# Local attention's probabilities: multiplied by the reciprocal of their sums on ScalarE instead of VectorE

## The reference

```python
# sliding_window_gqa_sinks, 16 query heads of 64, 2 key heads, window 128, two blocks of 128 queries
s = jnp.where(mask[None, :, None, None], s, -jnp.inf)
m = jnp.maximum(jnp.max(s, axis=-1, keepdims=True), sink)
p = jnp.exp(s - m)
p = p / (jnp.sum(p, axis=-1, keepdims=True) + jnp.exp(sink - m))
o = jnp.einsum("bnhgqk,bnkhd->bnqhgd", p.astype(vb.dtype), vb)
```

## Time and profile before

| | us |
|---|---|
| median of 3 runs (2653.89 to 2655.39) | 2654.91 |
| the profiled execution | 2654.99 |
| its span, first to last instruction | 2653.3 |
| TensorE busy | 2593.8 (98% of the span) |
| TensorE's weight loads busy | 2282.8 (86%) |
| VectorE busy | 1715.2 (65%) |
| ScalarE busy | 1275.3 (48%) |

### The profile page before, as it was taken

How to read it: one execution, slowest core, us unless ns; L and a number is a source line. 1 busy time by engine, 2 the same in 40 slices (tenths; PEclk the granted TensorE clock), 3 DMA queues, 4 the chain that set the end, 5 groups by cost and what they waited for, 6 DMA issues and landing times.

```text
span 2653.3 us, 40305 instructions
## 1 busy us (share of the span) xinstructions
PE 2593.8 (98%) x14812; PEld 2282.8 (86%) x14812; DVE 1715.2 (65%) x2239; ACT 1275.3 (48%) x1803; POOL 28.6 (1%) x50
## 2 busy tenths in 40 slices
PE   8999999998999999999999999999999999999998
PEld 8998889888977899999999988878888888888886
DVE  5778888885886755455556565467865555555654
ACT  5656454565557444343454444454444444444443
POOL 1000000000000000000000000000000000000000
PEclk9999999999999999999999999999999999999999
DMA  6565878774675556555567776658875656666664
GB/s 208 169 206 159 272 214 246 239 232 135 201 236 190 183 178 188 168 174 185 171 210 252 248 230 194 195 186 266 284 246 184 188 186 191 186 190 189 206 192 141
DMA packets 453112, 538.62 MB, mean 203 GB/s; under 512 B 33307, under 2 KB 344118, under 8 KB 452342
## 3 DMA queue, kind: packets, MB, share of 16 engines
q1 hardware_dynamic: 449430, 522.47, 62.7%
q0 software_dynamic: 3360, 14.31, 1.7%
q10 hardware_dynamic: 192, 0.08, 0.0%
HBM read 534.66 MB, written 2.10 MB: 202 GB/s over the span
## 4 chain that ended last, share of the span: by engine, by line
PE 88%; DVE 5%; ACT 2%; DVEq 2%; issue 1%; DMA 1%; ACTq 0%; SPq 0%
PE banks L2138 21%; PE banks L2139 20%; PE banks L2141 20%; PE banks L2123 7%; PE banks L2126 7%; PE banks L2124 6%; DVE w_lo L1385 2%; PE banks L2587 1%; DMA w_raw<-in_l_w_in 1%; PE banks L2327 1%; DVEq L1376 1%; PE banks L2629 1%; PE banks L2644 1%; PE banks L2567 1%; ACT w_hi L766 1%
## 5 line engine op out<-in xcount | busy, mean ns | idle before, releaser
L1385 DVE TENSOR_TENSOR w_lo<-w_raw,w_hi 128x1024 fp32r<-128x1024 f32 (+2 forms) x840 | 975.4, 1169 | 628.9 <-ACT w_hi L766 598.3
L766 ACT ACTIVATE w_hi<-w_raw 128x1024 fp32r<-128x1024 f32 (+2 forms) x840 | 843.3, 1013 | 908.3 <-PE banks L2141 751.9
L2138 PE MATMUL banks<-w_hi,act_hl 128*128 128x512 f32 (+2 forms) x2496 | 963.0, 386 | 8.2 <-DVE act_hl L1450 2.2
L2139 PE MATMUL banks<-w_hi,act_hl 128*128 128x512 f32 (+2 forms) x2496 | 957.2, 384 | 0.0
L2141 PE MATMUL banks<-w_lo,act_hl 128*128 128x512 f32 (+2 forms) x2496 | 692.9, 383 | 0.0
L2138 PEld LDWEIGHTS banks<-w_hi,act_hl 128*128 128x128 f32 x2496 | 471.1, 189 | 99.2 <-issue 3.7
L2139 PEld LDWEIGHTS banks<-w_hi,act_hl 128*128 128x128 f32 x2496 | 472.0, 189 | 82.8 <-issue 0.2
L2141 PEld LDWEIGHTS banks<-w_lo,act_hl 128*128 128x128 f32 x2496 | 456.9, 189 | 82.9
L2123 PE MATMUL banks<-act_hl,w_hi 128*128 128x256 f32 x1696 | 444.4, 293 | 8.8 <-ACT scr_a L772 2.5
L2124 PE MATMUL banks<-act_hl,w_hi 128*128 128x256 f32 x1696 | 429.6, 284 | 0.0
L2123 PEld LDWEIGHTS banks<-act_hl,w_hi 128*128 128x128 f32 x1696 | 324.4, 191 | 20.0 <-issue 9.6
(11 more groups left out here) (317 smaller groups left out, 1600.2 us busy)
## 6 DMA issues: line engine op xcount, KB each, us to landing
w_raw<-in_od_w_in SPq DMA_DIRECT2D x256, 512.0 KB, 3.9
w_raw<-in_ev_w_in SPq DMA_DIRECT2D x256, 256.0 KB, 3.7
w_raw<-in_l_w_in SPq DMA_DIRECT2D x96, 512.0 KB, 4.3
w_raw<-in_l_w_in SPq DMA_DIRECT2D x128, 256.0 KB, 3.8
ada_ring<-in_ada_w SPq DMA_DIRECT2D x128, 256.0 KB, 4.4
w_raw<-in_l_w_out SPq DMA_DIRECT2D x64, 512.0 KB, 4.8
y_mix<-in_ada_w SPq DMA_DIRECT2D x128, 256.0 KB, 3.2
const_b<-in_ada_w SPq DMA_DIRECT2D x128, 256.0 KB, 4.7
```

The costliest lines, as they stand in the source:

```text
L766: last = nc.scalar.activation(dst(w_hi[:, p % RING, :]), src(w_raw[:, p % RING, :]), ACT.Copy)
L1385: last = tt(dst(w_lo[:, p % RING, :]), src(w_raw[:, p % RING, :]), dst(w_hi[:, p % RING, :]).bitcast(F32), ALU.subtract)
L2138: mm(out, ah, hi, start=start, stop=False, skip_group_check=True)
L2139: r = mm(out, al, hi, start=False, stop=False, skip_group_check=True)
```

## The change

For each block ScalarE first runs the exponentials of both pairs as before. Then comes a drain, and for each pair a wait for its reciprocals and four copies in place with a scale that is read per partition from `soft`: for each head one of 128x128 and one of 128x256, eight copies a block. The last one signals that the probabilities are ready. VectorE adds the sink's term and takes the reciprocals, signals them for each pair, and no longer multiplies; its two multiplies a pair, four a block, go. No DMA and no matmul is added, removed or moved in the programs.

```diff
-            "swa": ("keys", "gate", "scores", "max", "exp", "prob", "probT", "probT_sb", "o", "y"),
+            "swa": ("keys", "gate", "scores", "max", "exp", "inv", "prob", "probT", "probT_sb", "o", "y"),
...
                     for n in range(2):
                         sc.wait_ge(s["max"], 2 * i + n + 1)
                         exps(swa_s, (2 * n, 2 * n + 1), s["exp"], True)
+                    nc.scalar.drain()
+                    probs = view(swa_s, 4, 384)
+                    for n in range(2):
+                        sc.wait_ge(s["inv"], 2 * i + n + 1)
+                        for h in (2 * n, 2 * n + 1):
+                            for b, (lo, hi) in enumerate(((0, 128), (128, 384))):
+                                last = copy(probs[:, h, lo:hi], probs[:, h, lo:hi],
+                                            scale=soft[:, 4, 2 * h + b:2 * h + b + 1])
+                    last.then_inc(s["prob"], 1)
...
                         drain()
-                        last = normalise(swa_s, (2 * n, 2 * n + 1))
-                    last.then_inc(s["prob"], 1)
+                        nc.vector.reciprocal(soft[:, 4, 4 * n:4 * n + 4], soft[:, 2, 4 * n:4 * n + 4]).then_inc(s["inv"], 1)
```

## The result

The changed kernel takes 2660.07 us (median of 20 runs, 2657.68 to 2662.98); the kernel before, on the same chip, 2655.64 us (20 runs, 2653.89 to 2658.43). The ratio is 1.0016, with a 95% interval from 1.001 to 1.0022: 4.4 us or 0.17% longer. The forecast was 2659.6 us. The profiled execution took 2661.22 us with a span of 2659.3 us and a mean granted clock of 0.992.

What follows compares the result with a forecast made beforehand. TensorE, busy 98% of the span, was taken as the bound, so only its waits or clock matter. The profiled 2654.99 + 3 x 0.97 for the longer chain + 1.7 for one clock fall gave 2659.6 us, range 2657.1 to 2661.9.

Steps and rivals of the forecast that it cites:

- Where the cost is paid: TensorE's waits before the transposes grow to 2.60, 2.00 and 2.24 us in blocks 2 to 4; block 1 costs nothing.
- The copies: ScalarE's eight scaled copies a block take 2.85 us, at the exponentials' 0.30 and 0.40 us each.
- The lower bound of 2.17: Least time in us for a block's eight ScalarE copies, from copies without a per-partition scale; +0.29 us a block.
- The drain, the reciprocals and the table load: On ScalarE: copies start 0.09 us after the exponentials, reciprocals are not late, no table load (rival with loads: chance 0.02).
- +0.97 a block: Transposes in blocks 2 to 4 start 0.97 us later each, bounds +0.29 and +1.60; +2.9 us over three blocks.
- the 0.6 us wait for `w_lo` in block 2 stays: TensorE's 0.6 us wait for a weight piece in block 2 lies before the multiplies, so it does not change.
- VectorE's relief counted at nothing: Removing four multiplies a block frees VectorE but not TensorE, whose next `w_lo` needs ScalarE's later `w_hi`: 0 us.
- What queues behind: ScalarE's next `w_hi` starts 2.95 us later, yet `w_hi` and `w_lo` arrive in time, by 0.4 and 0.3 us: no cost.
- The clock: TensorE's clock halves behind the longer waits of blocks 2 to 4, about a half each; likeliest once, 1.7 us, chance 0.37.
- the row without a fall and the one with it: Earlier TensorE waits: 2.47 us before 621.69 without a halved clock, 2.17 us with clock 0.50 from 644.45 to 647.86.
- none of today's waits is followed by a fall: In blocks 2 to 4 of the kernel before, TensorE's three waits, 1.63 us at most, were followed by no halved clock.
- The sum: Whole kernel: 2654.99 + 3 x 0.97 + 1.7 = 2659.6 us, +4.6 us or +0.17%.

Runs made afterwards that it cites:

- experiment 7: The changed kernel with a constant scale of 0.125 in the eight copies instead of the reciprocals: 2657.15 us, ratio 1.0004 to the kernel before.
- experiment 9: The changed kernel with ScalarE signalling each pair of copies, so TensorE transposes the first pair during the second's copies: 2658.11 us, ratio 1.0009 to the kernel before.
- experiment 10: The kernel before with one head of the second pair copied on ScalarE and transposes by pairs: 2653.83 us, ratio 0.999; on another chip 2655.0 us, ratio 0.9994.
- experiment 3: The changed kernel with 11, 8 and 9 unread matmuls filling TensorE's waits in blocks 2, 3 and 4: 2658.01 us, ratio 1.0007 to the kernel before.

## Why the prediction was right

**Where the cost is paid: right.** The waits are 2.60, 2.00 and 2.24 us, as foreseen to 0.01. Changing block 1 alone cost nothing; doubling its copies made a wait there.

**The copies: right.** 2.87 us against 2.85, from the pitch of the exponentials with the same operand kind. The lower bound of 2.17 came from copies without the scale per partition, and such copies took 2.13 (experiment 7).

**The drain, the reciprocals and the table load: right.** 0.08 against 0.09 us; the second pair's reciprocals are there at 266.42, about 1 us before their copies start (an estimate: half of 2.87 us after 266.05); no load.

**+0.97 a block: right, but the sum over the blocks was 0.35 too large.** The step that failed is the sentence that the 0.6 us wait for `w_lo` in block 2 stays, with VectorE's relief counted at nothing. The wait does lie before block 2's multiplies, but block 1's lie before the wait. That wait fell to 0.28. VectorE's timeline shows where it comes from, first in the kernel before,

```profile
197.57 0.75 DVE L1374 SCALAR_TENSOR_TENSOR acc_x<-ada_ring,silu_c,acc_x 128x512 f32<-128x512 f32 x1
198.76 1.23 DVE L1385 TENSOR_TENSOR w_lo<-w_raw,w_hi 128x1024 fp32r<-128x1024 f32 x1 [0.44 <-issue]
```

then in the changed one:

```profile
196.77 0.75 DVE L1383 SCALAR_TENSOR_TENSOR acc_x<-ada_ring,silu_c,acc_x 128x512 f32<-128x512 f32 x1
197.61 1.23 DVE L1394 TENSOR_TENSOR w_lo<-w_raw,w_hi 128x1024 fp32r<-128x1024 f32 x1
```

A gap of 0.44 us before a `w_lo`, in which VectorE waits for nothing that the profile shows, is gone. Counted from block 1's transposes, the sum before the gap starts at 15.16 us before and 15.17 after, and the `w_lo` behind it at 16.35 and 16.01; the `w_lo` for which TensorE waits starts at 26.59 and 26.25, so the 0.34 stay. The gap is gone in all eight profiles in which the whole of block 1's division is on ScalarE, and it is there (0.44 or 0.45) in the six others, the two with a single head on ScalarE among them. So the distance from block 1 to 2 grew by 0.63 and not by 0.97, and the path's cost is 0.63 + 0.97 + 0.98 = 2.6 us instead of 2.9. Why the gap depends on four multiplies 20 us earlier was not tried and stays open.

**What queues behind: right.** No wait for `w_hi` or `w_lo` followed in the changed kernel: the `w_hi` behind block 4's copies ended at 269.87, and TensorE's weight matmuls began at 270.26, so the 0.4 us to spare were there. They are also all there is: with 0.64 us less of transposes in the way (experiment 9) the same `w_hi` was 0.3 us late. After block 2 the last `w_lo` ended 39.92 us after block 1's transposes, where 40.28 was worked out; the difference is the same 0.35.

**The clock: the mechanism right, its shape and price a little off.** One fall was foreseen as likeliest, about half a chance per wait. Three profiles with the full set of waits (the changed kernel twice, and block 1's copies twice) show one fall each, in 9 waits of 2.0 to 2.6 us. Ten waits of 1.0 to 1.9 us in four profiles (before, block 1 alone, constant scale, and block 1 with its copies twice) have one between them, and the wait that experiment 9 splits has one as well. The half was a guess: the forecast said that the new waits lie between the row without a fall and the one with it, but there the fall is behind the shorter wait (2.17) and not behind the longer (2.47), and only 2.24 lies between them. The price was put at 1.7 us and is 1.4 to 1.5, by the distances. The step that failed is that none of today's waits is followed by a fall, which rested on one profile: block 1 alone had a fall behind 1.63 us, and filling the waits of the kernel before brought about 1.6 us. So the change does not bring one fall where there was none; it makes more of them. The Trainium skill (TensorE: Matmul & The Clock Gate, "What's actually happening") says that the point at which the clock changes varies from run to run. The traces agree: the same wait of 1.63 us has a fall in one and none in another.

**The sum.** 2.6 us of path, 0.2 outside the span, and added falls of 1.1 us by the fillers (2.7 less 1.6) or 1.7 by the granted clock make 3.9 or 4.5 of the measured 4.4. The forecast's 2.9 + 1.7 = 4.6 came out as close as it did partly by luck: the path's term was 0.3 too large, the 0.2 outside the span were in no term, and the 1.7 was meant as the price of one fall where there had been none, and stands now for 1.2 more of them at a lower price. The split of the 4.4 us between path and clock is firm for the path, where traces give it to 0.05 us as far as block 4, and loose for the clock, where only means over many runs do. That the path's 2.6 us reach the end of the kernel was not followed in the traces. The means of the filled kernels speak for it: 1.5 us above the kernel before on one chip and 1.6 below on another, so 3.0 apart, give or take 1.4.

## What to carry to other kernels

Before moving work to a less busy engine, look at which chain ends the wait of the engine that bounds: eight small in-place copies with a scale per partition made it 3.01 us from the last exponential to the transposes, where VectorE's four wider multiplies, half of them beside the exponentials, had made it 2.03. The same chain was shortened at no cost by signalling halves and letting the bound engine start on the first. With all copies on ScalarE half of that gain was lost again (experiment 9), and with two copies there all of what they were to add (experiment 10), since ScalarE's next piece came late. So look at what is next in line, at the weight loads too, before counting a shorter chain in full. Waits of TensorE of the size seen here (1.6 to 2.6 us) can cost more than their length: fill them with matmuls, sized to the wait, and judge by filled against unfilled runs, since a single profile shows one draw of the clock.

## What the runs showed that was not expected

- Matmuls whose result nobody reads made the changed kernel 2.7 us faster, with a higher granted clock (experiment 3).
- TensorE's clock fell behind a wait of 1.63 us in one execution and not in another, and in one execution it fell behind 2.24 us but not behind 2.61.
- An fp32 filler of 116 columns is shown as two matmuls of 0.11 us each (28 in 3.1 us for 14 fillers).
- A wait of 0.3 us for `w_hi` that the view of PE's waits does not list stands at the weight loads (experiments 9 and 10).
- Taking four multiplies from VectorE in block 1 removed a gap of 0.44 us without a releaser about 20 us later, which was worth 0.35 us on the path.
